# A two-block layer kernel on one Trainium2 core: the MLP's sums of weight blocks, moved from VectorE to loads that add

## What is computed

```python
def second_block(x, c, g_norm1, w_in, g_q, g_k, rel_bias, w_o, g_norm2, w1, w2, w_ada, b_ada):
    ...
    for l in range(DEPTH):
        mod = c_act @ w_ada[l] + b_ada[l]
        sh1, sc1, gt1, sh2, sc2, gt2 = [m[:, None, :] for m in jnp.split(mod, 6, axis=-1)]
        ...
        x = x + gt1 * (mixed @ w_o[l])
        h = rmsnorm_2(x, g_norm2[l]) * (1.0 + sc2) + sh2
        x = x + gt2 * (jnp.square(jax.nn.relu(h @ w1[l])) @ w2[l])
    return x
```

## Time and profile before

| | before |
|---|---|
| median of 3 runs | 984.08 us (982.9 to 984.8) |
| the profiled execution's own time | 980.84 us |
| its span | 979.1 us |
| TensorE busy | 959.3 us (98%) |
| VectorE busy | 712.2 us (73%) |
| ScalarE busy | 539.3 us (55%) |
| GpSimd busy | 70.0 us (7%) |

### The profile page before, as it was taken

How to read it: one execution, slowest core, us unless ns; L and a number is a source line. 1 busy time by engine, 2 the same in 40 slices (tenths; PEclk the granted TensorE clock), 3 DMA queues, 4 the chain that set the end, 5 groups by cost and what they waited for, 6 DMA issues and landing times.

```text
span 979.1 us, 13153 instructions
## 1 busy us (share of the span) xinstructions
PE 959.3 (98%) x4712; PEld 798.2 (82%) x4712; DVE 712.2 (73%) x1293; ACT 539.3 (55%) x1053; POOL 70.0 (7%) x158
## 2 busy tenths in 40 slices
PE   8999999999999999999999999899999999999998
PEld 7878998878888888777787878798888788878886
DVE  6487888868788759767678886956845883794773
ACT  6458787753222345489887664346645544644520
POOL 4000001011122012100000000100000000000000
PEclk9999999999999999999999999999999999999999
DMA  8205222239897524635434224215153052124201
GB/s 303 79 23 186 66 76 87 84 142 338 294 316 286 175 108 183 247 84 164 125 103 130 65 65 172 87 44 129 65 187 111 4 215 86 44 92 166 86 33 54
DMA packets 34082, 129.83 MB, mean 133 GB/s; under 512 B 8905, under 2 KB 8905, under 8 KB 24418
## 3 DMA queue, kind: packets, MB, share of 16 engines
q1 hardware_dynamic: 23538, 98.27, 29.5%
q0 software_dynamic: 7408, 26.75, 8.0%
q10 hardware_dynamic: 3072, 3.98, 1.2%
HBM read 119.45 MB, written 5.27 MB: 127 GB/s over the span
## 4 chain that ended last, share of the span: by engine, by line
PE 82%; DVE 9%; ACT 4%; issue 2%; DMA 2%; POOL 0%; SPq 0%; ACTq 0%; DVEq 0%; POOLq 0%
PE psum L2082 24%; PE psum L2083 24%; PE psum L2084 24%; PE psum L2249 3%; PE psum L2228 2%; PE psum L2278 2%; PE psum L2281 1%; DVE wl L1227 1%; DMA raw<-in_wall 1%; DVE two L1766 1%; DVE hl L1267 1%; DVE two L1631 1%; DVE xt L1263 1%; DMA value_rows<-rows 0%; PE psum L2511 0%
## 5 line engine op out<-in xcount | busy, mean ns | idle before, releaser
L2082 PE MATMUL psum<-hh,wh 128*128 128x512 f32 (+1 forms) x720 | 274.0, 380 | 0.7 <-DVE hl L1267 0.6
L2084 PE MATMUL psum<-hh,wl 128*128 128x512 f32 (+1 forms) x720 | 267.3, 371 | 0.0
L2083 PE MATMUL psum<-hl,wh 128*128 128x512 f32 (+1 forms) x720 | 267.2, 371 | 0.0
L688 ACT ACTIVATE wh<-raw 128x512 fp32r<-128x512 f32 x328 | 189.5, 621 | 89.6 <-PE psum L2084 41.7
L1227 DVE TENSOR_TENSOR wl<-raw,wh 128x512 fp32r<-128x512 f32 x328 | 213.7, 683 | 32.3 <-ACT wh L688 31.9
L2082 PEld LDWEIGHTS psum<-hh,wh 128*128 128x128 f32 x720 | 135.3, 188 | 24.5 <-DVE hl L1267 1.5
L2084 PEld LDWEIGHTS psum<-hh,wl 128*128 128x128 f32 x720 | 135.2, 188 | 23.9
L2083 PEld LDWEIGHTS psum<-hl,wh 128*128 128x128 f32 x720 | 135.5, 188 | 20.9 <-issue 1.0
L2082 PE MATMUL psum<-wh,ah 128*128 128x512 f32 x224 | 88.6, 396 | 0.7 <-issue 0.4
L2084 PE MATMUL psum<-wh,al 128*128 128x512 f32 x224 | 87.3, 390 | 0.0
L2083 PE MATMUL psum<-wl,ah 128*128 128x512 f32 x224 | 87.3, 390 | 0.0
(11 more groups left out here) (334 smaller groups left out, 1644.9 us busy)
## 6 DMA issues: line engine op xcount, KB each, us to landing
raw<-in_wall SPq DMA_DIRECT2D x75, 1024.0 KB, 5.2
wa<-in_wada POOLq DMA_DIRECT2D x24, 512.0 KB, 5.9
gt<-in_wada POOLq DMA_DIRECT2D x20, 512.0 KB, 7.2
xt<-in_xcols SPq DMA_DIRECT2D x8, 264.0 KB, 7.8
cb<-c_rows SPq DMA_DIRECT2D x8, 264.0 KB, 3.4
x<-in_x SPq DMA_DIRECT2D x4, 512.0 KB, 10.3
x_kept<-x SPq DMA_DIRECT2D x4, 512.0 KB, 2.8
sgt<-in_rel SPq DMA_DIRECT2D x8, 256.0 KB, 3.4
```

Source lines behind the costliest of these rows:

```text
L688: e.activation(home(w)[0][:, 512 * c:512 * c + 512], raw_of(w, c), ACT.Copy).then_inc(a["wh"], 1)
L2082: e.matmul(out_, lh, rh, start=start, stop=False, skip_group_check=True)
L2083: e.matmul(out_, lh, rl, start=False, stop=False, skip_group_check=True)
L2084: return e.matmul(out_, ll, rh, start=False, stop=stop, skip_group_check=True)
```

## The change

The combined weight blocks are no longer made by VectorE. The signs of the scheme are turned so that each combination is a plain sum: P7 uses b22+b12, P6 b22+b12+b11, P5 b11+b12, P4 b22+b12+b11+b21. A sum arises in a raw buffer: SP's queue loads the first block as before, and a load on GpSimd's queue with `accum_op=ALU.add` adds the next block from memory to what lies in the buffer. In each of quarters 0 to 2 there are five such adding loads of 1 MB, and nine plain loads in place of eight (b22 comes three times: as the base of P7, as the base of P6 and P4, and for P3). The signs are made good on the other side: the arguments of the VectorE instructions in `halves` and `blocks` are turned, and their number stays. The raw buffers of a quarter are called a0 to a3; in quarter 0, a0 is `raw3`.

```diff
-            def weight_sum(q, p):
-
-                b11, b22, b12, b21 = (W_MLP + 8 * q + 4 + i for i in range(4))
-                dst, x_, y_, op = {7: (b12, b22, b12, ALU.subtract), 6: (b11, b12, b11, ALU.add),
-                                   5: (b12, b22, b11, ALU.subtract), 4: (b11, b21, b11, ALU.subtract)}[p]
...
-                    e.tensor_tensor(raw_at(dst)[:, part], raw_at(x_)[:, part], raw_at(y_)[:, part], op).then_inc(v["wt"], 1)
...
-                    if r == 0:
-                        weight_sum(q, 7)
-                    elif r in (1, 2, 4):
-                        weight_sum(q, {1: 6, 2: 5, 4: 4}[r])
```

On SP's queue:

```diff
+            for q in range(4):
+                o, u, (a0, a1, a2, a3) = W_MLP + 11 * q, W_MLP + 8 * q, places[q]
+
+                if q:
+                    e.wait_ge(v["wl"], 4 * o + 4)
+                load(u + 4 + (1 if q < 3 else 0), a0)
+                e.wait_ge(v["wl"], 4 * (o + 1) + 4)
+                load(u + 4 + 1, a1)
+                e.wait_ge(v["wl"], 4 * (o + 2) + 4)
+                load(u + 4 + (0 if q < 3 else 2), a2)
+                e.wait_ge(v["wl"], 4 * (o + 3) + 4)
+                load(u + 4 + 3, a3)
+                if q < 3:
+                    e.wait_ge(v["wl"], 4 * (o + 5) + 4)
+                    load(u + 4 + 1, a3)
+                    e.wait_ge(v["wl"], 4 * (o + 6) + 4)
+                    load(u + 8, a0)
+                    e.wait_ge(v["wl"], 4 * (o + 8) + 4)
+                    load(u + 9, a2)
+                    e.wait_ge(v["wl"], 4 * (o + 9) + 4)
+                    load(u + 10, a3)
+                    e.wait_ge(v["wl"], 4 * (o + 10) + 4)
+                    load(u + 11, a1)
```

On GpSimd's queue, behind `gate(1)`:

```diff
             gate(1)
+
+            def add(q, m, i):
+
+                e.dma_start(raw_at(i), wall[W_MLP + 8 * q + 4 + m], accum_op=ALU.add).then_inc(d[f"wa{i}"], 16)
+
+
+            for q in range(3):
+                o, (a0, a1, a2, a3) = W_MLP + 11 * q + 4, places[q]
+                e.wait_ge(d[f"w{a0}"], 16 * n_load[o + 2])
+                add(q, 2, a0)
+                e.wait_ge(d[f"w{a1}"], 16 * n_load[o + 3])
+                add(q, 2, a1)
+                e.wait_ge(d[f"wa{a1}"], 192 + 16 * n_add[o + 3] - 16)
+                add(q, 0, a1)
+                e.wait_ge(v["wl"], 4 * o + 4)
+                add(q, 2, a2)
+                e.wait_ge(v["wl"], 4 * (o + 3) + 4)
+                add(q, 3, a1)
```

In `upper` on ScalarE, the wait on `wt` becomes one on the adding load:

```diff
-                    n, loaded = unit_of(w)
-                    if w and loaded:
-                        e.wait_ge(d[f"w{place[n]}"], 16 * nth[n])
-                q, m = divmod(w - W_MLP, 11)
-                if 0 <= q < 3 and m > 3 and PRODUCTS[m - 4] > 3:
-                    e.wait_ge(v["wt"], n_wt(q, PRODUCTS[m - 4]) + c // 2 + 1)
+                    if w:
+                        e.wait_ge(d[f"w{place[w]}"], 16 * n_load[w])
+                        if n_add[w]:
+                            e.wait_ge(d[f"wa{place[w]}"], 192 + 16 * n_add[w])
```

More of the change, by code:

```diff
@@ L316, in program @@
                  "ml", "tile", "mod", "ada", "x1", "yk", "xn1", "t1", "hl", "vca", "qn", "ql", "kl", "vsb", "x2", "xn2", "t2",
-                 "s", "sl", "wt", "x3", "score", "max", "rcp", "scan_s", "dv", "turn", "o", "oz", "ol")
+                 "s", "sl", "x3", "score", "max", "rcp", "scan_s", "dv", "turn", "o", "oz", "ol")
         g = sems("pool_", "const", "hm", "rs0", "rs1", "rs3", "mask", "bt", "strip")
@@ L328, in home @@
             return wh[:, w % NH, :], wl[:, w % NH, :]
[L332 to L349, removed]
@@ L351, in raw_at @@
-        def raw_at(n):
-            return raw3[:, :] if place[n] == 3 else raw[:, place[n], :]
-        def unit_of(w):
-            q, m = divmod(w - W_MLP, 11)
[L357 to L360, removed]
+        place = {w_: w_ % NR for w_ in range(W_MLP + 4)}
+        places = [(3, *(place[W_MLP + j] for j in range(1, 4)))]
@@ new lines, in program @@
+        for q_ in range(4):
+            a0, a1, a2, a3 = places[q_]
+            o_ = W_MLP + 11 * q_ + 4
+            place.update(zip(range(o_, o_ + 11), (a2, a3, a0, a1, a2, a3, a1, a0, a2, a3, a1) if q_ < 3 else places[q_]))
+            places.append((a0, a2, a3, a1))
+        n_load, n_add, loaded_, added_ = {}, {}, [0] * 4, [0] * 4
+        for w_ in range(NW):
+            q_, r_ = divmod(w_ - W_MLP - 4, 11)
+            p_ = PRODUCTS[r_] if 0 <= q_ < 3 and r_ < 7 else 0
+            loaded_[place[w_]] += p_ not in (4, 5)
+            added_[place[w_]] += {7: 1, 6: 2, 5: 1, 4: 1}.get(p_, 0)
+            n_load[w_], n_add[w_] = loaded_[place[w_]], added_[place[w_]] if p_ > 3 else 0
@@ L362, in raw_of, with raw_at @@
         def raw_of(w, c):
-            return raw_at(unit_of(w)[0])[:, 512 * c:512 * c + 512]
-        def n_wt(q, p):
-            return 8 * q + 2 * {7: 0, 6: 1, 5: 2, 4: 3}[p]
+            cs = slice(512 * c, 512 * c + 512)
+            return raw_at(place[w])[:, cs]
+        def raw_at(i):
+            return raw3[:, :] if i == 3 else raw[:, i, :]
         def n_sl(q, m, part):
@@ L558, in _, with load @@
             todo = [1]
+            def load(unit, i):
+                e.dma_start(raw_at(i), wall[unit]).then_inc(d[f"w{i}"], 16)
             def loads_to(last):
-                while todo[0] <= min(last, len(units) - 1):
+                while todo[0] <= min(last, W_MLP + 3):
                     n = todo[0]
@@ L564, in loads_to @@
                     if n >= NR:
[L565 to L568, removed]
+                        e.wait_ge(v["wl"], 4 * (n - NR) + 4)
+                    load(n, place[n])
             for kt in range(8):
@@ L670, in _ @@
                 e.dma_start(x2[:, i, :], kept[i]).then_inc(d[f"x{i}"], 16)
-            loads_to(len(units))
+            loads_to(W_MLP + 3)
+            for q in range(4):
[20 more added lines that the diff above has]
+                    load(u + 11, a1)
         @block.scalar
@@ L1830, in halves @@
                 y, c = tmp[:, m % 2, :], 16 * q + 3 * m - 8
-                e.tensor_tensor(f[:, 512:768], f[:, 512:768], y[:, 256:512], ALU.add).then_inc(v["s"], 1)
+                e.tensor_tensor(f[:, 512:768], y[:, 256:512], f[:, 512:768], ALU.subtract).then_inc(v["s"], 1)
                 e.wait_ge(v["s"], c + 1)
-                e.tensor_tensor(f[:, 0:256], f[:, 512:768], f[:, 0:256], ALU.subtract).then_inc(v["s"], 1)
+                e.tensor_tensor(f[:, 0:256], f[:, 512:768], f[:, 0:256], ALU.add).then_inc(v["s"], 1)
                 e.wait_ge(v["s"], c + 2)
-                e.tensor_tensor(f[:, 256:512], y[:, 0:256], f[:, 0:256], ALU.subtract).then_inc(v["s"], 1)
+                e.tensor_tensor(f[:, 256:512], f[:, 0:256], y[:, 0:256], ALU.subtract).then_inc(v["s"], 1)
             def hidden_lower(n, part=0):
@@ L1879, in blocks @@
                 dst, x_, y_, after = {
-                    "u2": (s6, s1, s6, (2, 5, b)), "u3": (s7, s6, s7, (3, "u2", b)), "c12a": (s6, s6, s5, (3, "u3", b)),
+                    "u2": (s6, s6, s1, (2, 5, b)), "u3": (s7, s6, s7, (3, "u2", b)), "c12a": (s6, s6, s5, (3, "u3", b)),
                     "c22": (s5, s7, s5, (3, "c12a", b)), "c11": (s1, s1, s2_, (3, "u2", b)),
                     "c12": (s6, s6, bank[P_BANK[3][b]], (3, "c12a", b)),
-                    "c21": (s7, s7, bank[P_BANK[4][b]], (3, "c22", b))}[name]
+                    "c21": (s7, bank[P_BANK[4][b]], s7, (3, "c22", b))}[name]
                 if name == "c12":
@@ L1886, in blocks @@
                 e.wait_ge(v["x3"], N_X3[after])
-                e.tensor_tensor(dst, x_, y_, ALU.add).then_inc(v["x3"], 1)
+                e.tensor_tensor(dst, x_, y_, ALU.add if name == "c11" else ALU.subtract).then_inc(v["x3"], 1)
             def add_block(ch, i):
```

## The result

The changed kernel takes 995.83 us in the median of 4 runs (995.25 to 996.86), against 984.44 us before, taken beside it (4 runs, 982.9 to 987.6). The ratio is 1.0113 with a 95% interval of 1.0086 to 1.0139: 11.4 us slower. The forecast was 998.1 us, with 986 to 1012 as its range. The profiled execution after took 995.43 us.

A forecast was written before the change was run, and what follows sets the result against it. TensorE, busy 98% of the span, was taken as the bound. Quarter 0 +15.8, clock +1.0, quarters 1 and 2 -2.8 made +14.0 us, on the median of 984.08 us 998.1 us, range 986 to 1012.

The forecast's parts named there:

- What bounds, and the gain: TensorE bounds the MLP; removing VectorE's sums wins 2.8 us in quarters 1 and 2, 3.45 us at most.
- 16 us: In quarters 1 and 2 an add may take up to some 16 us before anything shows.
- The place of the loss: Quarter 0: adds behind gate(1) make P7 start at 702.4 instead of 694.2 and P6 at 715.9.
- The price of one add, d = 5.4: Transfer engines' time for one 1 MB adding load: 5.4 us, against 2.7 for a plain load.
- Rival A: Cheap adds in quarter 0, d about 2.7 without sharing: 986.3 us; chance 0.17.
- B: Slow adds in quarter 0, d of 8.1 or more: 1008.9 us; chance 0.25.
- The start of the chain: Quarter 0: gate(1) waits for gate_rows until 688.78, and the gate's load lands at 692.9.
- the allowance of up to 2.7 us: Quarter 0: one plain load fewer beside the gate_rows transfers; nothing taken off, up to 2.7 us allowed.
- The clock: Half-speed matmuls after TensorE's stalls in quarter 0: from nothing to 5.4 us for P6, taken as 1 us.
- +15.8: Loss in quarter 0 from the late adds for P7 and P6: 15.8 us.
- C: Adds start early in quarter 0, as gate_rows' transfers land 2.7 us earlier; with d = 2.7, 983.6 us; chance 0.06.
- D: TensorE is bound elsewhere, so quarters 1 and 2 give no 2.8: 1000.9 us; chance inside the forecast's 0.52.

The follow-up runs named there:

- e6: The kernel before with its 24 weight sums cut to 8 columns each, all waits kept; 980.77 us against 983.74, ratio 0.9974.
- e1: The changed kernel with gate(1) moved behind quarter 0's first three adding loads on GpSimd's queue; 980.32 us against 984.35 for the kernel before, ratio 0.9965.
- e9: The changed kernel run once more, unaltered, on another chip; 1001.92 us, where the kernel before took 988.0 us, ratio 1.0134.
- e8: The changed kernel with SP's third load of b22 in quarter 0 held until P6's lowers are done; 999.79 us, ratio 1.0109 to the kernel before.
- e7: The changed kernel with 20 and 44 additional small matmuls in front of P7 and P6 of quarter 0; 1000.65 us, ratio 1.0121 to the kernel before.
- e2: The changed kernel with gate(1) between quarter 0's first adding load (P7's) and the second; 992.19 us, ratio 1.0070 to the kernel before.
- e3: The changed kernel without P6's second adding load in quarter 0, the gate still in front; 991.53 us, ratio 1.0078 to the kernel before.
- e5: The changed kernel with its 15 adding loads made plain ones on the same queue; 990.54 us against 983.74 for the kernel before, ratio 1.0065.
- e4: The changed kernel with 8 and 22 additional small matmuls in front of P7 and P6 of quarter 0; 995.66 us, ratio 1.0117 to the kernel before.

## Why the prediction was right

**What bounds, and the gain.** Right. TensorE lost 3.45 us in the products before. The 2.8 us forecast for quarters 1 and 2 came as 2.6, and e6 gives them to VectorE's sums alone. The adds were in time there: those issued from 783 us on landed in 7.7 to 8.2 us, and TensorE has no wait in these quarters. None took anything like 16 us, so that bound was not tried. VectorE's busy time on the page fell by 25.9 us where 29.2 were forecast, which changes nothing as VectorE isn't the bound. Its timeline after has idle time where the earlier trace rows had none:

```profile
796.81 0.68 DVE L1869 TENSOR_TENSOR sum_y<-sum_y,psum 128x512 f32<-128x512 f32 x1
799.17 0.69 DVE L1869 TENSOR_TENSOR sum_y<-sum_y,psum 128x512 f32<-128x512 f32 x1 [1.68 <-PE psum L2093]
```

**The place of the loss.** Right: GpSimd's adds behind `gate(1)`, P7 late, P6 late by the two adds in a row, P5 and the rest not. e1 moves one instruction and gets all of it back. The split was off: the forecast had TensorE stand still for 8.2 us before P7, and it was 3.5 (up to 5.7 in e9), partly because the chain started earlier, partly because the plain load fell on another add (both below).

**The price of one add, d = 5.4.** Right within the accuracy of the case. In e1 one add ran almost alone. Its queue's share of the 9.5 us from 640.5 to 650:

```profile
q0 software_dynamic: 144, 1.05, 61.8%
```

This is 0.618 x 9.5 = 5.9 us of the engines, and it landed after 8.1; I had 5.4 and 7.5. The kernel before has, from 647 to 652, for one plain load:

```profile
q1 hardware_dynamic: 140, 1.02, 58.7%
```

That is 0.587 x 5 = 2.9 us. An add costs the engines twice a plain load. The Trainium skill (Collectives: The Full Stack, section "The bandwidth ceiling: the fold count and why AG ≠ RS ≠ AR") says for the additions of a reduction that two source reads halve the rate. The trace agrees, with 5.9 us against 2.9. Rival A falls with this, and B too. Counted from the landing of the gate's load, P7's sum was there after 6.4 us, P6's first add 7.0 later and its second 8.0 after that, where the forecast had 8.1, 5.4 and 8.1: 21.4 us against 21.6. The plain load in between fell less on P7's add and more on P6's first than I had put it.

**The start of the chain** was off. I let the gate's load land at mark + 9.6, as before; it was issued at mark + 1.1 in place of + 5.4 and landed 5.5 us later, at mark + 6.6. So the allowance of up to 2.7 us for the missing plain load, which I didn't take, should have been taken and was even a little too small. The transfers into `gate_rows` have one 1 MB load beside them and not two, and the slower of them landed after 10.6 us and not 14.9. In the nine profiles with the changed order of loads it took 10.6 to 12.3 us, in the two with the former one 14.9 and 17.9 (e6). That the load beside them is the reason fits but wasn't tried alone. P6 started at mark + 29.5, forecast + 32.6 (715.9 - 683.3), and this accounts for nearly all of the 3.1 us.

**The clock** was undersized: 2.4 us, where I took 1.0. Across the executions it cost 1.8 (e9) to 3.2 us (e8) in P6. That the clock falls when TensorE stands still was right: it was granted at 0.88 in the mean of quarter 0 in the changed kernel and at 1.00 in e7. The that I read it from show only the start of a fall (0.92), not the half speed that I took from them; that stands first in the profile after. The Trainium skill, TensorE: Matmul & The Clock Gate, section "What's actually happening", says that the lower clock is the array's state when idle and that activity lifts it. These rows agree.

**The sum.** Forecast in the profile: +15.8 + 1.0 - 2.8 = +14.0. Measured there: +12.5 (the stall before P6, less the 0.7 of before) + 2.4 - 2.6 = +12.3. The two misses, 3 us too late a start and 1.4 us too little for the clock, partly cancel, and that is luck: with the clock sized right the forecast would have been 3.1 us over. On the medians the loss is 11.4 us where 14.0 were forecast. The third plain load of b22, for which I added 2.7, cost 1.3 to 1.9 us between the first two adds and 2.9 in all (e8 against e9).

**The rivals.** C saw the early gate rightly, but not that adds would be dear. D fell with the marks 43.6 us apart. What I didn't see in e2 is that relieving one step moves SP's plain loads into the same stretch, and in e3 that P5's add stays behind a wait for another product. On the medians e2 came out 4.1 to 6.5 us worse than I had worked out, e3 3.6 and e5 2.0 to 4.4.

## What to carry to other kernels

Work moved to a queue takes its place behind what stands there already: before adding to a queue, look at what the instruction ahead of it waits for, and put what has an early deadline in front. Loads that add cost the transfer engines twice a plain load and two into one target are chained here through their semaphores, so give each chain its full length (here 8 us a link, and up to 12 beside plain loads) ahead of its use. Relief of an engine that isn't the bound is worth only the stalls of the one that is: 25.9 us off VectorE were worth 2.6.

## What the runs showed of the hardware

- TensorE's granted clock can fall after a short halt: in the changed kernel it was at half within 4 us of P2's end, and in e4 it fell just after an idle time of 3.27 us, when matmuls ran again. Such a start of P6 cost 1.8 to 3.2 us. Small matmuls whose results nobody uses kept it up in e7.
- Adding loads move 180 to 220 GB/s at full DMA share (e2, 702 to 706 us: 180 and 184; the changed kernel, 710 to 716: 201 to 221), where plain loads moved over 400 (e5, 692 to 698 us: 418 to 426).
- Transfers of 2 KB in 4-byte pieces from ScalarE took up to 10.6 us to land in the changed kernel, with one 1 MB load beside them, and up to 14.9 before, with two; a plain load beside them took 14.5 us before, against 4.8. What share each has in the other's delay was not tried.
